# Attention results kept in SBUF, the mask moved into the product, and the scoring products in another order

## The chip, the cores and the metric

The kernel runs on one core of one Trainium2 chip. The metric is the device time in microseconds of one execution; lower is better. All data are float32.

## The reference, cut to what matters

One step of a one-layer encoder: 1024 new prompt rows and 32 sample rows with 128 cached keys. Three attention branches, a gated merge, an output projection, then PEER, which scores 128x128 product keys for each of 8 heads, keeps the best 16 experts of each row and head, gathers their rows of two tables (4 KB each) and sums them.

```python
def _mla_attend(...):                      # 8 heads, 64 + 32 dims
    s = (einsum(q_nope, k_nope) + einsum(q_rope, k_rope)) * MLA_SCALE
    s = where(k_pos // 64 <= q_pos // 64, s, -1e30)
    return einsum(softmax(s), v)

def _diff_attend(...):                     # 8 heads, two softmax maps each
    s = einsum(q, k) * DIFF_SCALE - slopes[h] * abs(q_pos - k_pos)
    s = where(chunk mask, s, -1e30);  p = softmax(s)
    return einsum(p[0] - lam * p[1], v)    # then an RMSNorm per head

def _mem_attend(...):                      # 4 heads, 256 memory tokens
    return einsum(softmax(einsum(q, mem_k) * MEM_SCALE), mem_v)

merged = g_a * (o_a @ w_br_a) + g_b * (o_b @ w_br_b) + g_m * (o_m @ w_br_m)
x = x + merged @ w_o

def _peer(h, ...):
    q = h @ wq;  sc = einsum(q, subkeys)   # (rows, 8 heads, 2 halves, 128)
    idx, g = top 16 of the 16 x 16 sums of each half's top 16, softmax
    a = gelu(einsum(u[idx], h));  return einsum(g * a, v[idx])
```

## The kernel before

Rows are worked on in tiles of 128; the sample rows are a ninth tile. `RUNS` makes three spans: tiles 0 and 1; tiles 2, 3, 4 and the sample; tiles 5, 6 and 7. Each span passes through the dense stages inputs, (memory, in the first span only), attend, merge, out and score. A stage opens on all engines when SP has seen that PE, ACT and DVE left the one before (`open_stage`, L545 and L546).

The experts are a second stream of 1056 steps, 16 for each group of 128 (row, head) pairs. In a step POOL gathers one row per partition from `peer_u` and one from `peer_v` (L594, 512 KB each, eight buffers for each table), DVE multiplies and sums (L1805), and every fourth step PE adds four weighted rows (L1968, `y_sum`). The ranking of the next group (`rank`, some twenty DVE instructions) is spread over the steps. POOL runs at most eight steps ahead of DVE and PE.

`weave` joins the two streams on PE, ACT and DVE: each dense generator yields once per tick, and after each tick the expert steps that are due by then are issued. `plan` works out how many steps are due from the costs in `ticks` and from a cap: in the scoring stage a group of 16 steps may begin only when the scores of its head are out. The first span has 21 steps in its scoring stage; the second span ends at step 321, the third at 736, and the rest runs alone.

Attention goes through jobs (pair of heads, branch, head, tile): 40, 80 and 60 in the three spans. For job j: PE writes scores to one of two PSUM buffers; DVE takes the row maximum (for the differential heads it adds the distance bias to SBUF and negates the maximum in an instruction of its own, L1356; for MLA it first writes -1e30 into a 64x64 corner, L1360); ACT takes exp; for differential heads DVE mixes the two maps; PE transposes, ACT copies to SBUF (L1297), PE multiplies by v (L1234), and `take_o` on DVE scales by the inverse sum (L1386, L1389). PE may write job j's product only when `take_o` of the job before has freed the bank (two banks in the first span). `copy_o` on ACT copies the transposed results of a pair of heads and issues their store to a DRAM scratch `oT` (L1315); SP waits for the last store before merge opens, and merge loads `oT` back beside `hT` (L1444, L1445). Two bias tables of 128x1024 are rescaled once for each pair of heads (L1429).

In the scoring stage a head's query product is two products of 256 rows of `peer_wq` columns (L1668), ACT copies each to SBUF (L1694), and then the sub-key products follow (L1679), which DVE copies out (L1709). The weights of a head (`w_q` 1 MB and `skT` 128 KB, one semaphore) have two buffers; the load for head h+2 is issued when head h's sub-key products are done:

```python
if h >= 2:
    eng.wait_ge(self.f_scored, self.f_sc0[i] + (h - 1) * sp.nt)
```

## Time and profile before

| | |
|---|---|
| median of 3 runs | 4473.66 us (4472.73 to 4478.42) |
| the profiled execution's own time | 4440.51 us, clock 0.761 |
| its span, first to last instruction | 4438.7 us |
| busy: PE, DVE, ACT, POOL | 2854.2, 2431.5, 807.9, 2377.4 us |
| DMA | 1388.83 MB, mean 313 GB/s |

The span splits into the pre-expert part (0 to 515 us), two parts in which dense stages and steps are woven (to 3400 us), and the steps alone (to 4438 us). Busy shares are averages over stages with different limits, so they are read by stage.

### The profile page before, as it was taken

What the parts mean: (1) busy time and instruction counts of PE and PEld (TensorE: products, weight loads), DVE (VectorE), ACT (ScalarE), POOL (GpSimd) and SP (SyncE); (2) the same over time, 40 slices, a digit from 0 to 9 for tenths busy, and PEclk for the clock granted to TensorE, in tenths of its full rate; (3) what the DMA queues carried; (4) which work ended last, traced back from release to release, by engine and by line L of the source; (5) the groups of instructions that cost most, each with busy time, mean ns of one, the idle gap of its engine ahead of it and who ended that gap; (6) DMA issues with size and microseconds to landing.
All of it is one profiled execution on the core that took longest, in us unless ns stands there. A gap on an engine that the chain in (4) does not pass through costs nothing.

```text
span 4438.7 us, 39034 instructions
## 1 busy us (share of the span) xinstructions
PE 2854.2 (64%) x12071; PEld 1509.4 (34%) x12071; DVE 2431.5 (55%) x6358; ACT 807.9 (18%) x1703; POOL 2377.4 (54%) x2128
## 2 busy tenths in 40 slices
PE   7779669777879965658667776896555332333333
PEld 5458445544445422334434333442222000000000
DVE  1241345377745445646488786655456565665650
ACT  1230012233321110112133332111001000000000
POOL 0000224355444346746466775675577777777774
PEclk9769879867689987879877787998777555555556
DMA  7244658788799789989899999998899999999997
GB/s 244 89 140 138 216 194 299 271 297 300 265 323 320 262 285 340 383 300 406 312 353 353 359 385 336 382 396 308 315 371 381 370 367 354 369 366 371 356 366 273
DMA packets 552141, 1388.83 MB, mean 313 GB/s; under 512 B 51296, under 2 KB 253024, under 8 KB 551936
## 3 DMA queue, kind: packets, MB, share of 16 engines
q0 software_dynamic: 304128, 1107.43, 67.1%
q1 hardware_dynamic: 227408, 249.27, 17.1%
q10 hardware_dynamic: 20400, 29.64, 2.0%
q8 instruction: 99, 1.62, 0.1%
q14 instruction: 106, 0.87, 0.1%
HBM read 1326.10 MB, written 60.05 MB: 312 GB/s over the span
## 4 chain that ended last, share of the span: by engine, by line
PE 34%; POOL 23%; issue 14%; DMA 12%; DVE 11%; ACT 2%; DVEq 2%; another core or an unknown queue 1%; SPq 1%; ACTq 0%; PEldq 0%; POOLq 0%; PEld 0%
POOL G_v_rows L594 12%; POOL G_u_rows L594 11%; PE scores L720 8%; PE scores L1479 7%; PE y_sum L1968 5%; DMA G_v_rows<-in_peer_v,G_idxT 4%; PE scores L1483 3%; DVE G_u_rows L1805 3%; PE scores L1565 2%; PE scores L1668 2%; PE o L1234 2%; DMA A_w_in<-in_w_in 2%; PE scores L1199 2%; DMA G_u_rows<-in_peer_u,G_idx 1%
## 5 line engine op out<-in xcount | busy, mean ns | idle before, releaser
L594 POOL DMA_INDIRECT G_v_rows<-in_peer_v,G_idxT x1056 | 1192.7, 1129 | 907.2 <-PE y_sum L1968 567.1
L594 POOL DMA_INDIRECT G_u_rows<-in_peer_u,G_idx x1056 | 1180.6, 1118 | 839.1 <-issue 308.2
L1805 DVE CUSTOM_DVE_ANT_0 G_u_rows<-G_u_rows,G_h 128x1024 f32<-128x1024 f32 x1056 | 1273.4, 1220 | 465.1 <-DMA G_u_rows<-in_peer_u,G_idx 420.3
L1968 PE MATMUL y_sum<-G_v_rows,G_zw 128*32 128x512 f32 x4224 | 782.9, 877 | 1000.1 <-DMA G_v_rows<-in_peer_v,G_idxT 945.6
L1968 PEld LDWEIGHTS y_sum<-G_v_rows,G_zw 128*32 128x32 f32 x4224 | 157.6, 140 | 1489.5 <-issue 1482.2
L720 PE MATMUL scores<-A_w_in,A_hT 128*128 128x256 f32 (+2 forms) x864 | 230.3, 428 | 45.0 <-DMA A_w_in<-in_w_in 30.0
L1479 PE MATMUL scores<-D_hT,D_w_gate 128*128 128x256 f32 (+2 forms) x768 | 237.5, 462 | 0.0
L720 PEld LDWEIGHTS scores<-A_w_in,A_hT 128*128 128x128 f32 x864 | 173.6, 204 | 104.0 <-DMA A_w_in<-in_w_in 27.0
L1217 PE MATMUL turn<-ident,C_probs 128*128 128x128 f32 (+1 forms) x647 | 144.0, 340 | 66.9 <-ACT C_pT L1297 44.0
L1479 PEld LDWEIGHTS scores<-D_hT,D_w_gate 128*128 128x128 f32 x768 | 144.5, 190 | 93.3 <-issue 56.1
L1709 DVE COPY F_sc<-scores 128x256 f32<-128x256 f32 x72 | 29.3, 422 | 255.8 <-PE scores L1679 184.7
L573 POOL MEMSET G_zw<- 128x1024 f32 x2 | 1.8, 957 | 293.4 <-SPq L546 293.4
L1217 PEld LDWEIGHTS turn<-ident,C_probs 128*128 128x128 f32 (+1 forms) x647 | 92.1, 178 | 168.6 <-issue 87.0
L1297 ACT ACTIVATE C_pT<-turn 128x512 f32<-128x512 f32 (+3 forms) x224 | 104.2, 465 | 242.6 <-PE turn L1217 164.9
L1479 PE MATMUL scores<-D_hT,DF_w 128*128 128x256 f32 (+2 forms) x384 | 125.3, 482 | 32.6 <-DMA D_hT<-scratch_hT 32.6
L1285 ACT ACTIVATE C_probs<-C_probs,C_ntop 128x768 f32<-128x768 f32 (+7 forms) x144 | 104.9, 729 | 212.8 <-DVE C_ntop L1356 165.9
L720 PE MATMUL scores<-A_hT,A_w_in 128*128 128x256 f32 (+2 forms) x384 | 133.4, 503 | 12.3 <-issue 12.3
L1234 PE MATMUL o<-C_v_diff,C_pT 128*128 128x64 f32 (+1 forms) x576 | 105.3, 344 | 55.9 <-DVE C_o_diff L1389 33.9
L1925 ACT ACTIVATE G_gelus<-G_dots 128x16 f32<-128x16 f32 x66 | 14.2, 216 | 677.1 <-DVEq L1809 536.9
L1668 PE MATMUL scores<-h2T,DF_w 128*128 128x256 f32 (+2 forms) x384 | 125.7, 487 | 16.2 <-DMA DF_w_br<-scratch_skT 15.8
L1512 DVE TENSOR_TENSOR D_part<-D_gate,scores 128x256 f32<-128x256 f32 (+2 forms) x48 | 25.0, 521 | 202.4 <-ACT D_gate L1498 158.9
L1668 PE MATMUL scores<-h2T,F_w_q 128*128 128x256 f32 (+2 forms) x384 | 123.7, 480 | 9.2 <-DMA F_skT<-scratch_skT 9.2
(282 smaller groups left out, 3923.5 us busy)
## 6 DMA issues: line engine op xcount, KB each, us to landing
A_w_in<-in_w_in SPq DMA_DIRECT2D x24, 1024.0 KB
D_w_gate<-in_w_gate SPq DMA_DIRECT2D x24, 1024.0 KB
G_u_rows<-in_peer_u,G_idx POOLq DMA_INDIRECT x1056
G_v_rows<-in_peer_v,G_idxT POOLq DMA_INDIRECT x1056
DF_w<-in_w_gate SPq DMA_DIRECT2D x12, 1024.0 KB
DF_w<-in_peer_wq SPq DMA_DIRECT2D x12, 1024.0 KB
F_w_q<-in_peer_wq SPq DMA_DIRECT2D x12, 1024.0 KB
G_sc<-scratch_sc ACTq DMA_DIRECT2D x66, 128.0 KB
```

The source lines that it names most:

```text
L594: pool.indirect_dma_start(out=buf[:, :], out_offset=None, in_=table, in_offset=bass.IndirectOffsetOnAxis(ap=rows, axis=0)).then_inc(signal ...
L720: last = pe.matmul(self.ps_m[n % 4][:, 0:width], lhs[c], rhs[c], start=(c == 0), stop=(c == len(lhs) - 1))
L1199: last = pe.matmul(self.ps_s[(slot + k) % 2][:, c:c + n], lhs, rhs, start=True, stop=True)
L1217: last = pe.transpose(ps_t[at % banks][0:w, b - c:b - c + P], probs[:, b:b + w], ident[:, :])
L1234: last = pe.matmul(ps_o[j % banks][:, 0:O_WIDTH[kind]], m["pT"][j % 2][0:w, b * P:(b + 1) * P], v, start=(b == 0), stop=(b == blocks - 1))
L1285: act.activation(probs[:, 0:keys], src[:, 0:keys], ACT.Exp, bias=m["ntop"][:, col:col + 1], accum_out=m["sums"][:, col:col + 1]).then_inc( ...
L1297: last = act.activation(m["pT"][j % 2][:, c:c + full], src[:, 0:full], ACT.Copy)
L1479: pe.matmul(gates[:, 0:n], m["w_gate"][b][:, c, block], m["hT"][:, c, :], start=(c == 0), stop=(c == DC - 1))
L1483: last = pe.matmul(branch[:, 0:n], m["w_br"][b][:, c, block], m["oT"][:, 4 * b + c, :], start=(c == 0), stop=(c == 3))
L1668: last = pe.matmul(self.ps_m[k % 2][:, 0:n], w[:, c, j * P:(j + 1) * P], m["h2T"][:, c, :], start=(c == 0), stop=(c == DC - 1))
L1805: dve.tensor_tensor_reduce(out=self.u_rows[slot][:, :], in0=self.u_rows[slot][:, :], in1=self.h2[t % 2][:, :], scale=1.0, scalar=0.0, op0= ...
L1968: last = pe.matmul(self.ps_y[32 * c:32 * (c + 1), cols], self.zw[b % 2][:, lo:lo + 32], self.v_rows[(4 * quad + c) % SLOTS_G][:, cols], st ...
```

## The change

- Results of attention are copied by ACT straight into the merge stage's `oT` in SBUF; the DRAM scratch, its stores, its load and SP's wait for it are gone.
- `take_o` moves from DVE to ACT. The reciprocal stays on DVE, is made for all jobs in `mix`, and waits there for the job's exp.
- The differential heads use one distance table for all heads: q is scaled by -DIFF_SCALE/slope when it is copied, the scores are shifted by the distance and scaled by the slope in one instruction that keeps the minimum, and exp is taken with scale -1. The rescaling of the bias tables and the separate negation are gone.
- The MLA mask becomes eight more rows of q and k (104 instead of 96 contraction rows); POOL makes them once and SP stores them to the scratches with 16 DMAs in the first input stage. The corner write is gone.
- In merge, out and score the ticks are finer (two per unit, three per tile, 24 instead of 16). The first three chunks of `w_o` lie elsewhere in SBUF and are loaded at the same place as before.
- In the scoring stage the first query product of head h+1 is issued ahead of the sub-key products of head h, on PE and on ACT. The load of head h+2 keeps its condition.

```diff
...
+MASKED = QK + SEQ // P
...
+def slope(h):
+    return 2.0 ** (-8.0 * (h + 1) / HEADS)
...
+            self.k_mask = self.B["subT"][0:KEY_TILES, :, :].rearrange("p b n -> p (b n)")[:, 0:KEYS]
+            self.q_mask = self.B["memT"][0:KEY_TILES, :, :, :].rearrange("p k c n -> p (k c n)")[:, 0:ROWS]
         self.experts_memory(keep)
-        with ExitStack() as ctx:
-            sb(ctx, "below_w_o", [P, BELOW_W_O])
-            self.w_o_head = [sb(ctx, f"E_w_o_head{k}", [P, D]) for k in range(W_O_HEAD)]
...
-        m["bias"] = [sb(ctx, f"C_bias{i}_{u}", [P, D]) for u in range(2)]
...
-            out += [(sp.i, "merge", 0.022 * sp.n)] * D_UNITS
-            out += [(sp.i, "out", 17.0)] * sp.nt
-            out += [(sp.i, "score", 0.016 * sp.n + 0.5 * sp.nt)] * (2 * HEADS)
+            out += [(sp.i, "merge", 0.0147 * sp.n), (sp.i, "merge", 0.0073 * sp.n)] * D_UNITS
+            out += [(sp.i, "out", 7.0), (sp.i, "out", 7.0), (sp.i, "out", 3.0)] * sp.nt
+            query, scores = (sp.i, "score", 0.016 * sp.n), (sp.i, "score", 1.0 * sp.nt)
+            out += [query] + [query, query, scores] * (HEADS - 1) + [query, scores]
...
-                out.append(max(0, min(steps, first + TOPK * max(0, heads // 2 - 1))))
+                out.append(max(0, min(steps, first + TOPK * max(0, (heads - 1) // 3 - 1))))
...
+        for u, top in ((1, P), (0, P // 2)):
+            for g in range(PAIRS):
+                pool.memset(self.q_scale[0:top, g:g + 1], -DIFF_SCALE / slope(2 * g + u)).then_inc(self.q_scaled, 1)
+            pool.wait_ge(self.q_scaled, PAIRS * (2 - u))
+        self.chunk_masks(pool)
...
+    def chunk_masks(self, pool):
+
+
+        pool.memset(self.k_mask, -1e30).then_inc(self.masks_zeroed, 1)
+        pool.memset(self.q_mask, 0.0).then_inc(self.masks_zeroed, 1)
+        pool.wait_ge(self.masks_zeroed, 2)
+        pool.affine_select(out=self.k_mask, in_=self.k_mask, compare_op=ALU.is_ge, fill=0.0, base=-CHUNK,
+                           pattern=[[1, KEYS]], channel_multiplier=-P).then_inc(self.masks_cut, 1)
+        pool.wait_ge(self.masks_cut, 1)
+        pool.affine_select(out=self.k_mask, in_=self.k_mask, compare_op=ALU.is_ge, fill=0.0, base=P - 1,
+                           pattern=[[-1, KEYS]], channel_multiplier=P).then_inc(self.masks_cut, 1)
+        for at, t in enumerate(ORDER):
+            if t < KEY_TILES:
+                rows = self.q_mask[:, at * P:at * P + CHUNK]
+                pool.affine_select(out=rows, in_=rows, compare_op=ALU.not_equal, fill=1.0, base=-t,
+                                   pattern=[[0, CHUNK]], channel_multiplier=1).then_inc(self.masks_cut, 1)
...
+            eng.wait_ge(self.masks_cut, 2 + KEY_TILES)
+            for h in range(HEADS):
+                eng.dma_start(s["kT"][h, QK:MASKED, :], self.k_mask).then_inc(self.masks_out, 16)
+                eng.dma_start(s["qT"][h, QK:MASKED, :], self.q_mask).then_inc(self.masks_out, 16)
...
-                take((name, u), m["flat"][k % 2][:, 0:sp.width], sp.width, DIFF_SCALE if name == "dq" else MEM_SCALE)
+                if name == "dq" and i == 0 and u == 0:
+                    act.wait_ge(self.q_scaled, 2 * PAIRS)
+                take((name, u), m["flat"][k % 2][:, 0:sp.width], sp.width, self.q_scale[:, u:u + 1] if name == "dq" else MEM_SCALE)
...
-                eng.dma_start(m["q_mla"][u][0:QK, :], s["qT"][2 * g + u, :, sp.cols]).then_inc(self.c_mla[u], 16)
-                load_keys(m["k_mla"][u], QK, s["kT"], 2 * g + u, self.c_mla[u])
+                eng.dma_start(m["q_mla"][u][0:MASKED, :], s["qT"][2 * g + u, :, sp.cols]).then_inc(self.c_mla[u], 16)
+                load_keys(m["k_mla"][u], MASKED, s["kT"], 2 * g + u, self.c_mla[u])
...
-        eng.wait_ge(self.c_oT_out, 48 * PAIRS * (i + 1))
...
+        def take_o(j):
+            g, kind, u, t, _, _ = jobs[j]
+            if g and j % o.n == 0:
+                act.wait_ge(self.c_turned, self.c_turn0[i] + o.o_turn[g - 1] + 3 * o.o_groups)
+            act.wait_ge(self.c_weighed, self.c_job0[i] + j + 1)
+            act.wait_ge(self.c_inverse, self.c_job0[i] + j + 1)
+            col, lo, w = 2 * (j % 4), 0 if kind == "mem" else VD * u, O_WIDTH[kind]
+            act.activation(m["o"][kind][:, sp.tiles.index(t), lo:lo + w], ps_o[j % outs][:, 0:w], ACT.Copy,
+                           scale=m["inv"][:, col:col + 1]).then_inc(self.c_taken, 1)
+
         def copy_o(g):
-            if g:
-                act.wait_ge(self.c_oT_out, 48 * (PAIRS * i + g))
             at = o.o_turn[g]
             for n, kind in enumerate(("mla", "diff", "mem")):
-                for c in range(o.o_groups):
-                    act.wait_ge(self.c_turned, self.c_turn0[i] + at + 1)
-                    k = min(o.BLOCKS, nt - o.BLOCKS * c)
-                    act.activation(m["oT"][kind][:, o.BLOCKS * c:o.BLOCKS * c + k, :].rearrange("p t n -> p (t n)"),
-                                   ps_t[at % banks][:, 0:k * P], ACT.Copy).then_inc(self.c_turn_out, 1)
-                    at += 1
-                act.wait_ge(self.c_turn_out, self.c_turn0[i] + at)
-                act.dma_start(s["oT"][g + PAIRS * n, :, sp.cols],
-                              m["oT"][kind][:, :, :].rearrange("p t n -> p (t n)")).then_inc(self.c_oT_out, 16)
+                act.wait_ge(self.c_turned, self.c_turn0[i] + at + n + 1)
+                act.activation(m["oT"][:, g + PAIRS * n, :], ps_t[(at + n) % banks][:, 0:sp.n], ACT.Copy).then_inc(self.c_turn_out, 1)
...
+            if j >= 2:
+                take_o(j - 2)
...
-                                             in1=m["bias"][u][:, lo:lo + keys], scale=1.0, scalar=-3.0e38,
-                                             op0=ALU.add, op1=ALU.max, accum_out=m["top"][:, col + k:col + k + 1]).then_inc(self.c_shifted, 1)
-                dve.drain()
-                dve.tensor_scalar(m["ntop"][:, col:col + 2], m["top"][:, col:col + 2], -1.0, None, ALU.mult).then_inc(self.c_maxed, 1)
+                                             in1=self.dist[:, lo:lo + keys], scale=slope(2 * g + u), scalar=HIGHEST,
+                                             op0=ALU.add, op1=ALU.min, accum_out=m["ntop"][:, col + k:col + k + 1]).then_inc(self.c_shifted, 1)
+                dve.drain().then_inc(self.c_maxed, 1)
                 return
-            src = self.ps_s[slot % 2]
-            if kind == "mla" and t < KEY_TILES:
-                dve.memset(src[0:CHUNK, keys - CHUNK:keys], -1e30)
-                dve.drain()
-            dve.tensor_reduce(m["ntop"][:, col:col + 1], src[:, 0:keys], AX, ALU.max, negate=True).then_inc(self.c_maxed, 1)
+            dve.tensor_reduce(m["ntop"][:, col:col + 1], self.ps_s[slot % 2][:, 0:keys], AX, ALU.max, negate=True).then_inc(self.c_maxed, 1)
...
         def mix(j):
             _, kind, _, _, keys, slot = jobs[j]
+            col, n = 2 * (j % 4), o.slots_of(j)
+            dve.wait_ge(self.c_exped, self.c_slot0[i] + slot + n)
+            dve.reciprocal(m["inv"][:, col:col + n], m["sums"][:, col:col + n]).then_inc(self.c_inverse, 1)
             if kind != "diff":
                 return
-            col = 2 * (j % 4)
             first, second = m["probs"][slot % 6], m["probs"][(slot + 1) % 6]
-            dve.wait_ge(self.c_exped, self.c_slot0[i] + slot + 2)
-            dve.reciprocal(m["inv"][:, col:col + 2], m["sums"][:, col:col + 2])
...
-        def take_o(j):
-            g, kind, u, t, _, _ = jobs[j]
-            col = 2 * (j % 4)
-            if g and j % o.n == 0:
-                dve.wait_ge(self.c_turned, self.c_turn0[i] + o.o_turn[g - 1] + 3 * o.o_groups)
-            dve.wait_ge(self.c_weighed, self.c_job0[i] + j + 1)
-            if kind != "diff":
-                dve.reciprocal(m["inv"][:, col:col + 1], m["sums"][:, col:col + 1])
-                dve.drain()
-            lo = 0 if kind == "mem" else VD * u
-            dve.tensor_scalar(m["o"][kind][:, sp.tiles.index(t), lo:lo + O_WIDTH[kind]], ps_o[j % banks][:, 0:O_WIDTH[kind]],
-                              m["inv"][:, col:col + 1], None, ALU.mult).then_inc(self.c_taken, 1)
...
-        def square_o():
-            dve.drain()
+        def square_o(g):
+            dve.wait_ge(self.c_taken, self.c_job0[i] + g * o.n + o.last["diff"] + 1)
...
-            if k >= -1 and (k + 1) % o.n == 0:
-                for u in range(2):
-                    dve.tensor_scalar(m["bias"][u][:, :], m["bias"][u][:, :], ALIBI_STEP, None, ALU.mult)
...
-        eng.dma_start(m["oT"][:, :, :], s["oT"].rearrange("c p n -> p c n")[:, :, sp.lo:sp.lo + sp.n]).then_inc(self.d_o, 16)
...
+            yield
             if unit == 0:
-                pe.wait_ge(self.d_o, 16 * (i + 1))
+                pe.wait_ge(self.c_turn_out, self.c_turn0[i] + C_OF[i].turns)
...
-        for h in range(HEADS):
-            w, skT, qT = m["w_q"][h % 2], m["skT"][h % 2], m["qT"][h % 2]
-            pe.wait_ge(self.f_w[h % 2], 32 * (HEADS // 2 * i + h // 2 + 1))
-            for j in range(2):
-                k = 2 * h + j
-                if k >= 2:
-                    pe.wait_ge(self.f_q_out, 2 * HEADS * i + k - 1)
-                for c in range(DC):
-                    last = pe.matmul(self.ps_m[k % 2][:, 0:n], w[:, c, j * P:(j + 1) * P], m["h2T"][:, c, :],
-                                     start=(c == 0), stop=(c == DC - 1))
-                last.then_inc(self.f_queried, 1)
-                if j == 0:
-                    yield
+
+        def query(h, j):
+            k = 2 * h + j
+            if j == 0:
+                pe.wait_ge(self.f_w[h % 2], 32 * (HEADS // 2 * i + h // 2 + 1))
+            if k >= 2:
+                pe.wait_ge(self.f_q_out, 2 * HEADS * i + k - 1)
+            for c in range(DC):
+                last = pe.matmul(self.ps_m[k % 2][:, 0:n], m["w_q"][h % 2][:, c, j * P:(j + 1) * P], m["h2T"][:, c, :],
+                                 start=(c == 0), stop=(c == DC - 1))
+            last.then_inc(self.f_queried, 1)
+
+        def scores(h):
+            skT, qT = m["skT"][h % 2], m["qT"][h % 2]
             pe.wait_ge(self.f_q_out, 2 * HEADS * i + 2 * h + 2)
             for t in range(nt):
                 k, r = h * nt + t, sp.rows[t]
@@ -1679,28 +1730,50 @@
                     last = pe.matmul(self.ps_m[2 + k % 2][0:r, j * P:(j + 1) * P], qT[:, j, t * P:t * P + r], skT[:, j, :],
                                      start=True, stop=True)
                 last.then_inc(self.f_scored, 1)
+
+        query(0, 0)
+        yield
+        for h in range(HEADS):
+            query(h, 1)
+            yield
+            if h + 1 < HEADS:
+                query(h + 1, 0)
+                yield
+            scores(h)
             yield
         pe.drain().then_inc(self.pe_left, 1)
...
```

## Rows read from the trace of the kernel before

**Rows 1.** Windows of seven stretches: us, busy us of each engine, granted clock, DMA share, GB/s.

```profile
...
183.00:296.00 113.00, 82.16 (x328) 59.68 (x328) 62.18 (x266) 53.32 (x176) 0.00 (x0) 0.61 0.25 74
...
850.00:1271.00 421.00, 313.78 (x1472) 183.66 (x1472) 311.00 (x926) 154.94 (x402) 211.79 (x192) 0.68 0.81 285
1271.00:1515.00 244.00, 229.92 (x784) 114.72 (x784) 108.89 (x258) 36.87 (x53) 107.43 (x100) 0.97 0.90 312
...
1594.00:1896.00 302.00, 175.95 (x736) 81.22 (x732) 168.96 (x426) 29.54 (x55) 197.97 (x167) 0.78 0.92 338
...
2184.00:2754.00 570.00, 413.89 (x2116) 224.60 (x2116) 458.91 (x1163) 195.42 (x380) 387.34 (x347) 0.75 0.98 358
2754.00:3023.00 269.00, 232.04 (x880) 118.34 (x880) 151.03 (x375) 45.75 (x67) 170.15 (x149) 0.94 1.02 379
...
3400.00:4438.00 1038.00, 324.53 (x1488) 62.42 (x1488) 572.21 (x1406) 76.19 (x147) 763.31 (x688) 0.57 0.96 356
...
```

**Rows 2.** Chain of waits, shares by line, of 183 to 296 us and 850 to 1271 us.

```profile
by line: issue 18.4%; ACT C_probs L1285 12.0%; DVE C_probs L1352 7.8%; DVE C_ntop L1362 6.3%; DVE C_probs L1376 6.0%; PE scores L1199 5.9%; ACT L1329 4.3%; DVE C_coef L1373 3.9%; DVE C_bias L1429 3.2%; DVE C_o_mla L1389 3.0%; DVE C_ntop L13
by line: issue 17.2%; PE o L1234 12.7%; PE y_sum L1968 12.6%; PE scores L1199 9.5%; DVE G_u_rows L1805 8.1%; PE turn L1217 5.7%; DVE C_probs L1352 3.8%; ACT C_probs L1285 2.5%; DVE C_probs L1376 2.5%; DVE C_ntop L1362 2.2%; PE turn L1249 1.
```

**Rows 3.** Groups by line in the whole run: busy, mean ns, idle before.

```profile
...
L1389 DVE TENSOR_SCALAR C_o_mla<-o,C_inv 128x64 f32<-128x64 f32 x64 | 18.1, 283 | 6.4 <-issue 1.7
...
L1386 DVE RECIPROCAL C_inv<-C_sums 128x1 f32<-128x1 f32 x108 | 16.8, 156 | 40.1 <-PE turn L1249 20.8 <-remote 7.9 <-issue 5.2
...
L1429 DVE TENSOR_SCALAR C_bias<-C_bias 128x1024 f32<-128x1024 f32 x24 | 15.5, 688 | 0.0
...
L1356 DVE TENSOR_SCALAR C_ntop<-C_top 128x2 f32<-128x2 f32 x72 | 13.1, 182 | 6.8
...
L1371 DVE RECIPROCAL C_inv<-C_sums 128x2 f32<-128x2 f32 x72 | 11.9, 166 | 42.3 <-ACT C_probs L1285 34.7 <-issue 6.6
...
L1389 DVE TENSOR_SCALAR C_o_mem<-o,C_inv 128x128 f32<-128x128 f32 x32 | 11.2, 351 | 2.5
...
L1300 ACT ACTIVATE C_pT<-turn 32x128 f32<-32x128 f32 x16 | 4.0, 250 | 0.0
...
```

**Rows 4.** Waits of PE in 850 to 1271 us: total, times, longest.

```profile
...
PE o L1234 <- DVE C_o_diff L1389: 23.1, 11, 5.5
PE o L1234 <- DVE C_o_mla L1389: 16.6, 5, 4.5
...
```

**Rows 5.** Waits of SP in the whole run: total, times, longest.

```profile
...
SPq L546 <- DMA scratch_oT<-C_oT_mem: 8.9, 3, 6.4
...
```

**Rows 6.** Timeline of PE in the first scoring stage: start, us, what.

```profile
...
483.27 7.07 PE L1668 MATMUL scores<-h2T,F_w_q 128*128 128x256 f32 x32
490.82 1.16 PE L1679 MATMUL scores<-F_skT,F_qT 128*128 128x128 f32 x8 [0.47 <-ACT F_qT L1694]
491.81 7.07 PE L1668 MATMUL scores<-h2T,DF_w 128*128 128x256 f32 x32
...
546.18 8.64 PE L1668 MATMUL scores<-h2T,F_w_q 128*128 128x256 f32 x32 [3.02 <-DMA F_skT<-scratch_skT]
...
```

**Rows 7.** Timeline of SP in the same stretch: issues of the sub-key loads.

```profile
...
483.88 0.58 SPq L1655 DMA_DIRECT2D DF_w_br<-scratch_skT  x1
...
534.06 0.58 SPq L1655 DMA_DIRECT2D F_skT<-scratch_skT  x1
...
```

**Rows 8.** Chain in order of time, 40 to 70 us.

```profile
...
50.92 14.99 DMA scratch_dqT<-A_flat
...
```

**Rows 9.** Timeline of SP in the first input stage.

```profile
...
52.77 0.43 SPq L658 DMA_DIRECT2D out_ckv<-A_kv  x1
...
```

**Rows 10.** Waits of PE from 466 to 1896 us.

```profile
...
PE scores L1679 <- ACT F_qT L1694: 34.2, 15, 24.1
...
```

**Rows 11.** Timeline of PE in the second scoring stage.

```profile
...
1689.40 3.59 PE L1679 MATMUL scores<-DF_w_br,F_qT 128*128 128x128 f32 x15 [3.13 <-ACT F_qT L1694]
...
```

152 lines of the change are left out of this document (97 added, 55 removed).

## The prediction

> **What bounds the kernel now.** I read the windows by stage first, then the chain of waits of single stages, the groups by line, the waits of one engine, and last the timeline where an order changes. The reader should see three kinds of stretch.
>
> The steps that run alone, 3400 us to the end, hold the DMA engines 96% busy at 356 GB/s [rows 1]. The change touches nothing there, so 1038 us stay.
>
> In the woven part the stages differ. Attention of the second span (850 to 1271 us) has the DMA at 0.81, PE busy 314 of 421 us at a mean granted clock of 0.68, DVE 311 us [rows 1]: no engine is full. Its chain goes back and forth between PE, DVE and "issue" [rows 2], and PE waits 39.7 us for DVE's `take_o` of MLA and differential jobs [rows 4]. Attention of the third span is another case: 570 us at a DMA share of 0.98, and merge behind it at 1.02 [rows 1]. There faster engines mostly wait for gathers. Merge of the second span is PE's: 229.9 of 244 us busy at clock 0.97 [rows 1]; finer ticks can't shorten it.
>
> Before the first gather nothing is DMA-bound. Attention of the first span (113 us, DMA 0.25) is a chain of short instructions [rows 1, 2], and every microsecond taken off that chain is a gain.
>
> **Part by part.** All terms are changes in us against the profiled execution's 4440.51 (span 4438.7). The median of the runs shown, 4473.66, is 33.2 above it (0.7%); I subtract the same microseconds from it.
>
> *DVE in attention.* Gone are `take_o` (0.28 us for 64 columns, 0.35 for 128), the negation (0.18) and the rescaling (0.69 each, ten a span with the first two) [rows 3]. The corner write has no row here; it is shorter than the smallest of these, so at most 0.18 for 24 jobs in each of the later spans. The reciprocal (0.16) stays. Removed from DVE: in the first span 40 x 0.3 + 16 x 0.18 + 10 x 0.69 = 22; in the second 80 x 0.3 + 32 x 0.18 + 6.9 + 4.3 = 41; in the third 60 x 0.3 + 24 x 0.18 + 6.9 + 4.3 = 33.
>
> *First span, -14.* A differential job runs around DVE, ACT and DVE, and a take of another job sits in that round with its reciprocal: 16 x (0.18 + 0.16 + 0.28) = 10, and the chain gives L1429 3.2% of 113 = 3.6 [rows 2, 3]. Bounds: -7 (only L1429 and the MLA take by their chain shares, 3.2% and 3.0%) and -22 (all).
>
> *Second span, -25.* The 41 us come off an engine that PE waits for. None of the removed lines is among the largest shares of this chain [rows 2], so they are not all on it; but the take holds PE's bank, and on ACT it comes ahead of the copy, where ACT (155 of 421 us busy [rows 1]) waits for PE anyway. Its price on ACT is bounded by 0.25 for a 32-row copy [rows 3]: 80 x 0.25 = 20 us on an idle engine, taken as hidden; without the cover it would cost those 20. Against it stands a new wait: DVE now waits for exp in 48 non-differential jobs too, and behind it in DVE's queue stand the next maximum, the expert steps and with them POOL. The row for differential jobs shows 42.3 us idle before 72 reciprocals, 0.59 each [rows 3], so at most 28 us here; in roughly half the ticks a step lies between and hides it, and I let 10 count. 41 x 0.85 - 10 = 25. Bounds: -41, and -8 (one line of 2% of the chain).
>
> *Third span, -12.* 33 us less DVE work, but only 2% of 570 = 11 us of DMA time is free; to this comes the store of 2.4 MB to `oT` (12 blocks x 128 x 384 x 4 bytes), 6.6 us at 358 GB/s [rows 1], less some wait for exp. Bounds -28 (share 1.02 as in merge, and the store) and -4.
>
> *Ends of attention, -9.* SP waited 8.9 us in total for the last stores before it opened merge [rows 5]. That goes; PE now waits for ACT's last copy, which it did before through the stage's end. The third wait, 6.4 of the 8.9, lies in the DMA-bound part, so bounds -13 (with the twelve store issues of ACT in the first span) and -4.
>
> *Merge and out, -4.* 6.5 MB of `oT` are no longer loaded; 2.4 MB of them in the stage at 1.02 are 6 us at 379 GB/s [rows 1], the others lie beside PE-bound work. Finer ticks give single microseconds in out. Bounds -12 and 0.
>
> *The mask rows.* 104 instead of 96 rows are loaded for q and k of MLA: 8 x 96 x 4 bytes x (512 + 1312 + 1408 columns) = 9.9 MB become 10.8; 0.8 MB at 358 GB/s is +2, bounds 0 and +2. The matmuls stream the same columns. The Trainium skill ("DMA: Bandwidth & Descriptors", section on why a DMA increments its semaphore by 16) says that a DMA of SP runs on the largest number of engines up to 16 that divides its slowest dimension. By that rule 96 rows use 16 engines and 104 rows 13, so the busiest engines carry a third more: 27.7 us become 37, +9 in place of +2, a rival below. No row here shows a 104-row load.
>
> *The mask's DMAs, +4.* In the first input stage 16 issues of 0.43 us [rows 9] go into SP's queue behind the memory loads and ahead of the first `dqT` store. They are 6.9 us on a queue where that store, issued at 50.92, is 14.99 us of the chain [rows 8]: ACT waits for it to reuse its buffer, and PE for ACT. Part of that landing time is the queue's backlog, which the delay doesn't lengthen. Bounds 0 and +8. POOL's mask work has no row; it lies beside 30 us of inputs.
>
> *The order of the scoring products, +18.* Here I expect a loss. The gain is PE's wait for ACT's copy: 0.47 us per head in the first span [rows 6], 34.2 us in all up to 1896 us, of which 24.1 are one stall by the first ranking, which stays [rows 10]. The cost is the cover of the weight load. The load of head h+2 is issued when head h's sub-key products end (483.88 us [rows 7]). Before, two products (7.07) and the next sub-key products (1.16) lay ahead of its first use at 491.81, which waited for nothing [rows 6]: the load took at most 7.9 us. Under gathers it took from 534.06 to 546.18, 12.1 us, and PE waited 3.02 [rows 6, 7]. After, only one product, 3.5 us, lies between. In the first span six loads are affected; that of head 4 falls into the 24 us stall. For the first two I take 7 us, for the last three 9.5 (between 7.9 and 12.1, nearer the lower as fewer gathers run in a slower stage): 2 x 3.5 + 3 x 6 = 25. After the wait of 3.02 the pair of products took 8.64 for 7.07 [rows 6], so 1 us more each: 30. Off go 8 x 0.47, the old stall of 4.6, and one product that is done ahead when the stall ends (3.5): +18. Bounds: all at 12.1 gives +39; loads of 5 us give +3.
>
> *Scoring in the second and third span, 0.* Sixteen steps lie behind most heads' sub-key products and cover the load. Only head 2's load is exposed, and the stretch without steps at the start is one product longer (about 6 us, POOL idle). Against it, waits as the 3.13 us for ACT in mid-stage go [rows 11]. The stage runs at a DMA share of 0.92 [rows 1]. Bounds -12 and +12.
>
> Sum: -14 - 25 - 12 - 9 - 4 + 2 + 4 + 18 = **-40**, so 4400.5 profiled and 4433.7 us for the median.
>
> **The rivals.** *Attention gains more* (all low bounds there): -22 - 41 - 28 in place of -51, hence 4394 us. Speaks for it PE's wait for the take [rows 4]; against, that the removed lines are small in the chain. Chance 0.12.
>
> *The DMA takes the gain*: if gathers refill every gap in the later spans, attention gives there only the store's bytes, 5.5 MB at 358 GB/s = 15 in place of 37, and with the 7 us of that in the second span half hidden, 25 less gain: 4459 us. For it the 0.98 of the third span, against it the 0.81 of the second [rows 1]. Chance 0.15.
>
> *The weight loads decide, slower than before*: the load of head h+2 arrives later than its one product in all spans. All at 12.1 in the first span is +21 over my term; in the later spans, if steps don't cover them, six loads each at 12.1 - 5.5 = 6.6 are up to +79, of which the steps hide half: 4434 + 21 + 40 = 4495 us. It turns the sign when loads add 58 us in all. For it [rows 6, 7]; against, the bursts of 16 steps. Chance 0.10.
>
> *The wait for exp decides*: 108 jobs x 0.59 = 64, all on the path in place of 10 to 15: 4434 + 51 = 4485 us. Against it, in the woven spans a step mostly lies between. Chance 0.06.
>
> *Thirteen engines for the mask rows*, the rule above: loads of 10.8 MB on the busiest engines, +7 over my term: 4441 us. Chance 0.07.
>
> **How the numbers follow.** My forecast has 0.50 and, with its bounds, 4400 to 4464. The range for 8 in 10 reaches over the other cases: 4388 to 4478. What this measurement can't tell from no change is 0.2%, about 9 us (4464.7 to 4482.6). Faster: 0.48 + 0.12 + 0.11 + 0.06 = 0.77. Same: 0.02 + 0.04 + 0.01 + 0.02 + 0.01 = 0.10. Slower: the rest, 0.13.
>
> **What would show it.** Right: the first attention near 99 us; the second at 390 to 400 with no wait of PE for a take; a wait of PE for `w_q` or `skT` before the first product of heads 2, 3, 5, 6 and 7 in the first scoring stage; merge opening at once when ACT has left; the last 1038 us unchanged. Wrong: an attention of the second span above 415 us, reciprocals on DVE that idle over 0.5 us each, or scoring of the later spans above 310 us with PE waiting for weights.

## The result, and the profile after

The changed kernel took 4439.66 us (median of 4 runs, 4430.28 to 4446.12), the kernel before 4473.19 us beside it: 33.5 us or 0.75% less. The ratio on record is 0.9922, with a 95% interval from 0.9901 to 0.9943. The prediction was 4433.7 us. On another chip, with eleven runs, the ratio was 0.9954 (0.9939 to 0.9968), 21.8 us. Its profiled execution has a span of 4428.6 us, only 10.1 less than the profiled one of before: that one ran 33 us under its kernel's median, this one 9. So the first pair of profiles shows where time went, and understates the sum.

The windows by stage of the changed kernel, the stretches that answer to [rows 1] (the same columns):

```profile
193.00:302.00 109.00, 80.80 (x334) 59.47 (x335) 43.13 (x184) 61.81 (x216) 1.85 (x2) 0.61 0.28 86
862.00:1258.00 396.00, 300.50 (x1472) 178.56 (x1472) 279.48 (x783) 172.74 (x482) 211.50 (x192) 0.71 0.85 300
1258.00:1492.00 234.00, 229.58 (x784) 114.58 (x784) 105.95 (x254) 35.58 (x52) 102.44 (x96) 0.98 0.88 304
...
2171.00:2732.00 561.00, 399.03 (x2116) 213.98 (x2116) 436.02 (x1053) 209.77 (x440) 399.38 (x348) 0.77 0.99 361
2732.00:2995.00 263.00, 231.93 (x880) 117.99 (x880) 147.22 (x363) 44.47 (x66) 160.59 (x147) 0.95 1.03 374
3390.00:4428.00 1038.00, 325.71 (x1488) 62.69 (x1488) 572.15 (x1407) 76.19 (x147) 749.90 (x686) 0.59 0.96 355
```

DVE has lost 31.5 us of work in the second span's attention (311.0 to 279.5), ACT gained 17.8. The stretches are shorter in attention, the same in the steps alone. The first window runs 2 us into merge, so attention 1 is better read from the table below. To see what each stage gave, I take from the timelines the first PE instruction of a stage and the first of the next. "c" is the pair that was profiled later on one other chip:

| stage | before | after | change | change, c |
|---|---|---|---|---|
| first inputs and memory | 175.2 | 184.2 | +9.0 | +7.5 |
| attention 1 | 117.6 | 104.5 | -13.1 | -12.5 |
| scoring 1 | 113.4 | 130.2 | +16.8 | +15.1 |
| attention 2 | 425.6 | 395.7 | -29.9 | -35.8 |
| scoring 2 | 310.9 | 326.6 | +15.7 | +10.5 |
| attention 3 | 576.3 | 562.3 | -14.0 | -5.5 |
| scoring 3, to PE's last product | 283.9 | 305.6 | +21.7 | +13.1 |
| merge and out, all three | 845.7 | 836.4 | -9.3 | -8.7 |
| inputs 2 and 3, start | 545.0 | 544.4 | -0.6 | +5.5 |
| steps alone | 1045.0 | 1038.6 | -6.4 | -15.3 |

Attention gave 57 us in the first pair and 54 in the second. Scoring took 54 and 39 of it back; 6 and 15 of that came off the steps alone, for the most part because the third scoring stage of the changed kernel holds more steps (in the second pair four: 688 matmul records of PE in it for 672). The second scoring stage holds the same steps as before, to within one. Single stages differ by up to 9 us between the two pairs (attention 3: -14.0 and -5.5).

PE's waits for the take in the second span's attention, to be read beside [rows 4] (total, times, longest):

```profile
PE o L1293 <- ACT C_o_diff L1370: 9.1, 6, 2.6
PE o L1293 <- ACT C_o_mla L1370: 8.4, 5, 3.0
PE o L1293 <- ACT C_o_mem L1370: 7.4, 3, 3.4
PE o L1293 <- issue: 17.1, 13, 4.8
```

The 39.7 us of MLA and differential jobs have become 17.5. Both views put a good part of PE's idle time ahead of this product to "issue", that is to nothing that they can name. In the kernel before this line reads:

```profile
PE o L1234 <- issue: 32.2, 13, 5.8
```

Taken together PE idled 77.3 us ahead of it before (with the 5.4 for memory jobs) and 42.0 now. The second pair, below, gives nearly the same sums, 78.8 and 41.4, and puts all of them to the take. So [rows 4] showed only half of this wait. The prediction's sign "no wait of PE for a take" didn't come: the wait has halved.

The groups by line that answer to [rows 3] (busy, mean ns, idle before):

```profile
L1426 DVE RECIPROCAL C_inv<-C_sums 128x1 f32<-128x1 f32 x108 | 17.2, 159 | 38.5 <-ACT C_probs L1344 30.8 <-issue 6.7
...
L1370 ACT ACTIVATE C_o_mla<-o,C_inv 128x64 f32<-128x64 f32 x64 | 19.4, 304 | 18.0 <-remote 12.6 <-PE o L1293 4.2 <-issue 1.0
L1370 ACT ACTIVATE C_o_diff<-o,C_inv 128x64 f32<-128x64 f32 x64 | 19.3, 302 | 32.5 <-remote 20.4 <-issue 6.4 <-PE o L1293 5.5
```

The take is 0.30 us on ACT where it was 0.28 on DVE. The reciprocals of the 108 jobs with one map now idle DVE for 38.5 us, 0.36 each, against the 0.59 of the differential ones in [rows 3]. Before, they idled it for 40.1 us, mostly for PE's turns [rows 3], so the new wait took the place of another and the total didn't grow.

The first scoring stage is where the prediction expected the loss. Timeline of PE (start, us, what, and in brackets the wait ahead of it), against [rows 6]:

```profile
482.31 3.62 PE L1718 MATMUL scores<-h2T,F_w_q 128*128 128x256 f32 x16
488.66 3.72 PE L1718 MATMUL scores<-h2T,DF_w 128*128 128x256 f32 x16 [2.73 <-DMA DF_w_br<-scratch_skT]
492.22 1.05 PE L1730 MATMUL scores<-F_skT,F_qT 128*128 128x128 f32 x8
493.11 3.62 PE L1718 MATMUL scores<-h2T,DF_w 128*128 128x256 f32 x16
499.61 3.72 PE L1718 MATMUL scores<-h2T,F_w_q 128*128 128x256 f32 x16 [2.89 <-DMA F_skT<-scratch_skT]
...
513.69 5.91 PE L1718 MATMUL scores<-h2T,DF_w 128*128 128x256 f32 x16 [6.01 <-DMA DF_w_br<-scratch_skT]
535.18 2.08 PE L1730 MATMUL scores<-F_skT,F_qT 128*128 128x128 f32 x8 [15.57 <-issue]
...
549.26 5.20 PE L1718 MATMUL scores<-h2T,F_w_q 128*128 128x256 f32 x16 [7.81 <-DMA F_skT<-scratch_skT]
...
561.60 5.41 PE L1718 MATMUL scores<-h2T,DF_w 128*128 128x256 f32 x16 [2.80 <-DMA DF_w_br<-scratch_skT]
...
574.20 3.72 PE L1718 MATMUL scores<-h2T,F_w_q 128*128 128x256 f32 x16 [2.84 <-DMA F_skT<-scratch_skT]
```

Every first product of heads 2 to 7 waits for its weights, 25.1 us in all. The 6.01 of head 4 lies in the stall by the first ranking: its product is done at 519.6, and the next one, at 535.18, needs the queries that ACT copies behind that ranking (timelines of DVE, which begins it, and of ACT):

```profile
508.67 0.49 DVE L1795 MAX8 G_best<-G_sc 128x8 f32<-128x128 f32 x2 [3.98 <-DMA G_sc<-scratch_sc]
```

```profile
534.76 0.64 ACT L1755 ACTIVATE F_qT<-scores 128x256 f32<-128x256 f32 x2
```

From the start of the ranking to this copy it is 26.1 us; in the kernel before it was 25.7, without any wait for weights (505.20 to 530.85). So head 4's load costs nothing, and 19.1 us of waits count. Counted from the stage's first product, head 3's sub-key products begin 7.3 us later than before (66.9 for 59.6), as head 2's and 3's waits and one more product now lie ahead of the ranking. The last product ends 13.7 later, and the next input stage begins 16.8 later: 3 us of the stage's growth lie behind its products.

SP issued two of these loads at:

```profile
482.51 0.37 SPq L1704 DMA_DIRECT2D DF_w<-in_peer_wq  x1
...
537.29 0.37 SPq L1704 DMA_DIRECT2D F_w_q<-in_peer_wq  x1
```

The first (head 2) was in use 6.1 us later, the second (head 5), under gathers, 12.0 us later; four of the six landed within 6.1 to 6.4.

And SP's queue in the first input stage, beside [rows 8, 9], with the step of the chain that follows:

```profile
57.74 0.51 SPq L700 DMA_DIRECT2D scratch_kT<-B_subT  x1
58.29 0.29 SPq L701 DMA_DIRECT2D scratch_qT<-B_memT  x1
58.63 0.35 SPq L727 DMA_DIRECT2D scratch_dqT<-A_flat  x1
```

```profile
58.63 17.48 DMA scratch_dqT<-A_flat
```

The store that was issued at 50.92 and took 14.99 us is issued 7.7 us later and takes 2.5 us longer. The 16 issues are 5.8 of the 7.7 (52.80 to 58.58); the queue was 1.8 behind before them. The chain names SP's mask issues one after the other from 52.80 on: they are on the path.

### The profile page after: what moved, and what is told of

Read it like the earlier page. It is cut to its first block, busy times and chain, and to the rows that moved or that the text cites. A ratio compares the mean times of both kernels' runs of the same rounds, so it can differ in the third digit from the quotient of the medians.

```text
span 4428.6 us, 38852 instructions
## 1 busy us (share of the span) xinstructions
PE 2830.5 (64%) x12071; PEld 1499.0 (34%) x12071; DVE 2352.5 (53%) x6012; ACT 846.4 (19%) x1881; POOL 2385.5 (54%) x2148
## 4 chain that ended last, share of the span: by engine, by line
PE 33%; POOL 26%; DMA 13%; issue 12%; DVE 7%; another core or an unknown queue 3%; ACT 2%; DVEq 1%; SPq 1%; ACTq 0%; PEldq 0%; POOLq 0%; PEld 0%
POOL G_v_rows L646 13%; POOL G_u_rows L646 13%; PE scores L778 7%; PE scores L1515 6%; DMA G_v_rows<-in_peer_v,G_idxT 5%; PE y_sum L2041 5%; PE scores L1520 3%; PE scores L1718 2%; PE scores L1258 2%; DVE G_u_rows L1878 2%; PE o L1293 2%; PE scores L1605 2%; DMA G_u_rows<-in_peer_u,G_idx 1%; DMA DF_w_br<-scratch_skT 1%
## 5 line engine op out<-in xcount | busy, mean ns | idle before, releaser
L646 POOL DMA_INDIRECT G_v_rows<-in_peer_v,G_idxT x1056 | 1176.5, 1114 | 929.5 <-PE y_sum L2041 561.5
L646 POOL DMA_INDIRECT G_u_rows<-in_peer_u,G_idx x1056 | 1194.3, 1131 | 813.0 <-issue 320.0
L608 POOL MEMSET G_zw<- 128x1024 f32 x2 | 1.9, 964 | 279.5 <-SPq L576 279.5
L1718 PE MATMUL scores<-h2T,F_w_q 128*128 128x256 f32 (+2 forms) x384 | 125.3, 481 | 17.5 <-DMA F_skT<-scratch_skT 17.4
L1420 DVE TENSOR_REDUCE C_ntop<-scores 128x1 f32<-128x256 f32 (+6 forms) x108 | 65.6, 607 | 119.6 <-PE scores L1258 99.1
```

Of the source, the lines that this page charges most:

```text
L646: pool.indirect_dma_start(out=buf[:, :], out_offset=None, in_=table, in_offset=bass.IndirectOffsetOnAxis(ap=rows, axis=0)).then_inc(signal ...
L1718: last = pe.matmul(self.ps_m[k % 2][:, 0:n], m["w_q"][h % 2][:, c, j * P:(j + 1) * P], m["h2T"][:, c, :], start=(c == 0), stop=(c == DC - 1))
```

## The experiments

All kernels were timed against the kernel before on their own chip (4384.7 to 4389.5 us there, 2% under the first chip), so ratios are compared, and stages within one chip where possible. Four kernels make the first group.

**The scoring stage undone.** `x_old_score` is the changed kernel with the four scoring functions, the ticks and the cap of before:

```diff
-            out += [query] + [query, query, scores] * (HEADS - 1) + [query, scores]
+            out += [(sp.i, "score", 0.016 * sp.n + 0.5 * sp.nt)] * (2 * HEADS)
-                out.append(max(0, min(steps, first + TOPK * max(0, (heads - 1) // 3 - 1))))
+                out.append(max(0, min(steps, first + TOPK * max(0, heads // 2 - 1))))
```

> The changed kernel with the scoring stage of the kernel before: its order of products, its two ticks per head and its cap; all else as changed. Between the two profiles the three scoring stages grew by 16.9, 15.8 and about 15 us, 48 in all. Theory 1, the new order costs this by itself: about 48 us off the changed kernel's 4440, so 4392. Rival, the longer stages only hold expert steps that other stages lost, and nothing is gained by going back in the later spans: only the first span's 17 us come off, 4423.

Ratio 0.9855 (0.9838 to 0.9872): 4323.1 us. By the ratios, 0.9922 and 0.9954, the changed kernel lies 29 to 43 us above this. So the scoring order with its ticks and its cap costs this much, between the rival's 17 and theory 1's 48, and less than the 54 of the first pair's stages, as part of the longer third stage comes back in the steps alone.

**The scoring stage alone.** `b_new_score` is the reverse edit on the kernel before.

> The kernel before with only the new scoring order, its three ticks per head and its cap. Theory 1: 4473 + 48 = 4521. Rival (only the first span pays): 4490.

Ratio 1.0066 (1.0053 to 1.0079), +29 us; the first scoring stage grew to 133.5 us. The cost is there without the rest of the change too. Both expected sizes were off, 48 too high and 17 too low: the first span doesn't pay alone, the later ones pay as well.

**The weight load released earlier.** In `x_split_load` the load of the query weights waits for head h's query products only. The sub-key load keeps its condition and has a semaphore of its own, for which PE now waits ahead of its sub-key products:

```diff
         if h >= 2:
+            eng.wait_ge(self.f_queried, 2 * HEADS * i + 2 * (h - 1))
+        eng.dma_start(m["w_q"][h % 2][:, :, :], ...).then_inc(self.f_w[h % 2], 16)
+        if h >= 2:
             eng.wait_ge(self.f_scored, self.f_sc0[i] + (h - 1) * sp.nt)
-        eng.dma_start(m["w_q"][h % 2][:, :, :], ...).then_inc(self.f_w[h % 2], 16)
-        eng.dma_start(m["skT"][h % 2][:, :, :], ...).then_inc(self.f_w[h % 2], 16)
+        eng.dma_start(m["skT"][h % 2][:, :, :], ...).then_inc(self.f_k[h % 2], 16)
```

> The changed kernel, but peer_wq's load for head h+2 waits only for head h's two query products (semaphore of its own), the sub-key load keeps its condition. The order of the products stays. The load is then covered by product, sub-key products and product, 8.2 us in the first span in place of 3.5. Theory 1a, the uncovered weight load is all of the cost: the first scoring stage goes back to about 114 us and the later ones to 284 and 300, so 4440 - 45 = 4395. Theory 1b, the load explains only the first span, and the later spans pay because steps and sub-key products fall otherwise (PE waited 12.9 and 16.2 us for DVE's copies of the scores there, against 2.7 and 3.7 before): about -15, 4425.

Ratio 0.9894 (0.9870 to 0.9917), 12 to 26 us under the changed kernel's: theory 1b's 15 and not 1a's 45. In the first span the waits of heads 2 to 5 are gone, those of heads 6 and 7 are still 2.80 and 2.67 us; timeline of PE, start of the same stretch:

```profile
481.87 3.62 PE L1720 MATMUL scores<-h2T,F_w_q 128*128 128x256 f32 x16
485.33 3.62 PE L1720 MATMUL scores<-h2T,DF_w 128*128 128x256 f32 x16
...
489.67 3.62 PE L1720 MATMUL scores<-h2T,DF_w 128*128 128x256 f32 x16
493.13 3.62 PE L1720 MATMUL scores<-h2T,F_w_q 128*128 128x256 f32 x16
```

**The mask's stores issued early.** In `x_mask_early` the 16 issues stand ahead of the third load of `w_in`, where SP is idle.

```diff
+        if i == 0:
+            eng.wait_ge(self.masks_cut, 2 + KEY_TILES)
+            for h in range(HEADS):
+                ...
         self.load_w_in(eng, sp, 2)
         self.load_w_in(eng, sp, 3)
```

> The changed kernel with the mask's 16 stores issued ahead of the third load of w_in, where SP stands idle from 18.4 to 32.1 us. Theory: the first input stage grew by 9.0 us because 16 issues take 5.8 us on SP's queue ahead of the first dqT store and that store lands later; then 4440 - 9 = 4431 and the stage ends near 129 us in place of 139. Rival: the masks' bytes delay other transfers wherever they are issued: no more than 2 us off.

The input stage shortened from 126.6 (`x_old_score`, same chip) to 118.4 us, and the `dqT` store is back within 1.4 us of where it was; chain of waits, 40 to 90 us:

```profile
52.35 14.29 DMA scratch_dqT<-A_flat
```

The ratio, 0.9927 (0.9914 to 0.9939), doesn't show the 8 us. The changed kernel's two ratios, from two other chips, are 0.9922 and 0.9954, 14 us apart, so how much of the 8 us reaches the end is open.

The kernels of all groups, leaving out the first chip, give the price of the scoring stage with its scatter (us; 3' is scoring 3 with the steps alone):

| | scoring 1 | scoring 2 | 3' |
|---|---|---|---|
| seven kernels with the order of before | 109.6 to 112.9, mean 111.4 | 298.2 to 304.7, mean 301.4 | 1298.4 to 1311.3, mean 1304.2 |
| four with the new order | 127.9 to 133.5, mean 130.7 | 310.8 to 316.9, mean 314.7 | 1309.1 to 1328.0, mean 1316.5 |
| `x_split_load` | 113.4 | 308.4 | 1309.4 |

The new order costs 19.3 + 13.3 + 12.3 = 45 us. With the load released earlier 2 + 7 + 5 = 14 are left. In the first span, then, the uncovered load is nearly all of it. In the later spans it is about half by one kernel, where the halves (6 and 7 us) are no larger than the scatter; the rest belongs to the order or to its ticks and cap, which were not separated. PE's waits for weights show no share of the load there: behind the first load of each span they are 0.5 and 4.1 us in `c_after`, 0 and 5.3 in `c_before`, 0 and 5.8 in `x_split_load`. One wait that took a place of its own there is PE's for DVE's copies of the scores, 12.9 us in the changed kernel's second span where it was 2.7, but in `x_mask_early` it is 3.8, and the stage is 11 us longer than in `x_old_score` all the same, so it isn't the cause. What costs the 13 and 12 us stays open.

The second group, on another chip.

> The changed kernel as it is, on one chip with the kernels of this group. In the first pair of profiles it took 10 us less than the kernel before, in the timed runs 33.5. Expected: a ratio of 0.992, and attention of the three spans shorter by 13, 30 to 38 and 14 to 27 us, scoring longer by 17, 5 to 16 and 15 to 20.

> The kernel before as it is, for a profile on the same chip. Expected: ratio 1.000; its stages, beside the changed kernel's of this group, tell how far the single stages of the first pair of profiles can be trusted.

Ratios 0.9954 and 1.0000. The stage table above has this pair in its last column: the profiled spans are 4383.9 and 4357.9, 26.0 apart, near the 21.8 of the timed runs. The stages are as expected but for the third span's, whose attention gave 5.5 us (14 to 27 expected) and whose scoring took 13.1 (15 to 20).

**The take back on DVE.** `x_take_dve` differs from the changed kernel in one instruction's engine, and with it in its place: on ACT the take stands ahead of the next copy, on DVE behind the next job's `mix`, where it stood before.

```diff
-            act.activation(m["o"][kind][...], ps_o[j % outs][:, 0:w], ACT.Copy,
-                           scale=m["inv"][:, col:col + 1]).then_inc(self.c_taken, 1)
+            dve.tensor_scalar(m["o"][kind][...], ps_o[j % len(ps_o)][:, 0:w],
+                              m["inv"][:, col:col + 1], None, ALU.mult).then_inc(self.c_taken, 1)
```

> The changed kernel with the scaling of attention's results (take_o) back on DVE, at the place it had before; reciprocals stay in mix, everything else as changed. Theory: in the first span, where the chain of short instructions runs through DVE, 40 takes of 0.3 us come back, +5 to +12; in the second span 80 takes, 24 us of DVE time, about half of it on the path, +12; third span, DMA-bound, +3: in all some 20 to 25 us slower than the changed kernel. Rival: PE waits for the take wherever it runs (in the changed kernel it waited 25 us for ACT's takes in the second span, before 45 us for DVE's), and the move is worth less than 8 us.

4393.55 us, ratio 1.0017 (0.9999 to 1.0034), 28.8 us above the changed kernel, somewhat more than the 20 to 25 expected: without this one part the change is worth nothing. Where it lies I had wrong: attention 1 +1.3 us, attention 2 +30.0 (386.2 to 416.2), attention 3 +0.8. PE's waits in attention 2, in this order: the kernel before, the changed one, the take on DVE:

```profile
PE o L1234 <- DVE C_o_mla L1389: 31.0, 12, 5.8
PE o L1234 <- DVE C_o_diff L1389: 28.5, 16, 5.5
PE o L1234 <- DVE C_o_mem L1389: 19.3, 8, 5.1
```

```profile
PE o L1293 <- ACT C_o_mem L1370: 18.9, 10, 4.8
PE o L1293 <- ACT C_o_diff L1370: 11.4, 10, 2.6
PE o L1293 <- ACT C_o_mla L1370: 11.1, 7, 3.0
```

```profile
PE o L1293 <- DVE C_o_diff L1432: 31.5, 17, 5.5
PE o L1293 <- DVE C_o_mla L1432: 30.1, 12, 5.1
PE o L1293 <- DVE C_o_mem L1432: 19.5, 9, 5.5
```

78.8, 41.4 and 81.1 us. The other removals took 13.5 us off DVE's busy time there (310.4 to 296.9), and with the take on DVE attention 2 is 416.2, against 422.0 before: they are worth 6 there, no more than such stages scatter. What PE waited for was not the 0.28 us of the take but its turn in DVE's queue. The longest wait, 5.53 us until 943.17, as DVE's timeline shows it (the lines left out are more of the same ranking, and small instructions of the next job's `mix`):

```profile
936.76 1.22 DVE L1879 CUSTOM_DVE_ANT_0 G_u_rows<-G_u_rows,G_h 128x1024 f32<-128x1024 f32 x1 [0.18 <-issue]
...
938.88 0.69 DVE L1830 TENSOR_TENSOR G_work<-ranks,G_partf 128x512 f32<-128x512 f32 x1
939.65 0.76 DVE L1835 TENSOR_TENSOR G_work<-G_work,G_pos1f 128x256 f32<-128x256 f32 x2
940.49 0.69 DVE L1837 TENSOR_REDUCE G_key<-G_work 128x32 f32<-128x512 f32 x1
...
941.95 0.88 DVE L1421 SCALAR_TENSOR_TENSOR C_probs<-C_probs,C_coef,C_probs 128x640 f32<-128x640 f32 x1
942.75 0.28 DVE L1432 TENSOR_SCALAR C_o_diff<-o,C_inv 128x64 f32<-128x64 f32 x1
```

An expert step, a piece of the ranking (938 to 941.4 us) and the next job's `mix` (to 942.75) stand ahead of the take, and PE has one bank only. Whether the take would do as well on DVE ahead of `mix` wasn't tried, so how much is the engine's and how much the place's is open. In the first span there are two banks and next to no steps, and no wait of PE is put to the take in either kernel. In the third PE waits 27.4 us for it on DVE and 9.2 on ACT, yet the stage is as long (550.9 and 550.1 us): its DMA share is 1.00 in both. The move is worth about 1 us in each.

**Both remedies.** `x_best` has scoring as before and the mask stores early.

> The changed kernel with the scoring stage of the kernel before and the mask's stores issued early. If the two gains add up: ratio 0.9855 less 9 us, 0.983 to the kernel before. Rival: the 9 us of the first input stage don't reach the end (the kernel with early stores alone had the ratio 0.9927, no better than the changed kernel's 0.9922), then 0.9855.

4319.37 us, ratio 0.9852 (0.9826 to 0.9878), and as `c_best` on the chip of the first group:

> The kernel x_best again (changed kernel, scoring as before, mask stores early), as the base of this group. Expected: ratio 0.985.

4318.33 us, 0.9842 (0.9824 to 0.9860): the two are 1.5 and 1.6% under the kernel before, and 1% under the changed one. The early stores again don't show clear of `x_old_score`'s 0.9855, as the rival has it.

The last group has `c_best` as its base.

> x_best with two edits that touch different stages, read by stage: (a) peer_wq's load for head h+2 waits only for head h's query products, with scoring in the old order; (b) DVE makes the reciprocal of the jobs of one softmax map half a job later, behind the next maximum, when their exp is done. (a): PE's remaining waits for weights in scoring go, 3 us in the first span, 0 to 5 in each later one. (b) Theory, the new wait for exp costs: attention -3 to -5 us in the first span, -10 in the second, 0 to -5 in the third. Rival: DVE has slack there, its wait only fills it, and attention stays within 2 us of the base's. Ratio to the kernel before 0.980 by the theory, 0.984 by the rival.

(a) is the split load in the old order, (b):

```diff
         def mix(j):
-            dve.wait_ge(self.c_exped, self.c_slot0[i] + slot + n)
-            dve.reciprocal(...).then_inc(self.c_inverse, 1)
             if kind != "diff":
                 return
+            invert(j)
...
             if j + 2 < len(jobs):
                 maximum(j + 2)
+            if j + 1 < len(jobs):
+                invert_late(j + 1)     # the jobs that are not differential
```

4311.07 us, ratio 0.9839 (0.9815 to 0.9863), not told apart from its base. Attention 104.1, 383.9 and 546.5 us against 104.1, 386.7 and 553.4; scoring 1 and 2 111.0 and 298.6 against 110.8 and 300.5. PE's waits for weights, but for the first load of each span, went from 5.7 us to 0.2. Two runs of the base's own code on two chips had 386.6 and 386.7, but 549.1 and 553.4 in the third span. So the wait for exp costs 0 in the first span, up to 3 us in the second, and what it costs in the third isn't told from scatter. The rival is nearer.

> x_best with the mask as before: -1e30 into the 64x64 corner on DVE, 96 rows of q and k, no mask rows made or stored. Theory: the mask in the product takes 0.18 us and a drain of DVE's path per MLA job: first attention +2, second and third +3 each, against one fewer store train in the first inputs, 0: in all +5 to +8, ratio 0.987. Rival: nothing measurable.

```diff
-MASKED = QK + SEQ // P
+MASKED = QK
+            if kind == "mla" and t < KEY_TILES:
+                dve.memset(src[0:CHUNK, keys - CHUNK:keys], -1e30)
+                dve.drain()
```

Nothing of the mask rows is made or stored, either. 4320.10 us, ratio 0.9857 (0.9840 to 0.9874) against 0.9842 (0.9824 to 0.9860), not told apart: the timed runs are with the rival. Attention 1 is 2.6 us longer, as the theory has it; 2 and 3 are 383.5 and 552.9, not longer. The mask in the product is worth those 2.6 us in the profiles; its 16 issues in SP's queue lengthened the first inputs there by three times as much.

> x_best with 112 rows of q and k instead of 104 (eight rows of zeros more, 0.8 MB more to load). By the rule in the Trainium skill's page DMA: Bandwidth & Descriptors, 104 rows run on 13 engines and 112 on 16: then the loads get shorter, the wait for the first k_mla falls under the base's and the stages of attention by up to 3 us each. Rival: the load runs on all engines either way, and 112 rows are 8% more bytes: attention 0 to 1 us longer in each span.

```diff
-MASKED = QK + SEQ // P
+MASKED = QK + 2 * (SEQ // P)
```

4312.51 us, ratio 0.9837 (0.9822 to 0.9852). PE's wait for the first `k_mla` is 39.1 us in three, the base's 39.2. The issues of the key loads themselves differ; from the tile's summaries (durations in ns, min/median/max), with 104, 96 and 112 rows (`c_best`, `x_corner2`, `x_rows112`):

```profile
L1178 SPq DMA_DIRECT2D C_k_mla<-scratch_kT x40: 365/377/1182, 185.6 to 2419.0; - x40
```

```profile
L1170 SPq DMA_DIRECT2D C_k_mla<-scratch_kT x40: 419/426/478, 184.5 to 2413.9; - x40
```

```profile
L1178 SPq DMA_DIRECT2D C_k_mla<-scratch_kT x40: 416/428/1493, 184.9 to 2410.0; - x40
```

A key load of 104 rows is issued in less time than one of 96 or of 112. A mask store takes 0.29 us with its 8 rows and 0.42 or more with the 16 rows of `x_rows112`. The loads of q don't show it as cleanly: with 96, 104 and 112 rows alike single ones take anything from 0.30 to 0.46 us. By the rule of the Trainium skill ("DMA: Bandwidth & Descriptors", section on why a DMA increments its semaphore by 16) 8, 104, 96 and 112 rows run on 8, 13, 16 and 16 engines; the issue times of stores and key loads rise in that order, 0.29, 0.377, 0.426, 0.428, which agrees with the rule, but no view here counts a load's engines. What thirteen engines cost isn't told: the wait for the first load is the same, attention 2 and 3 are 380.2 and 547.1 with 112 rows against 386.7 and 553.4, 6 us each in one profile, and the median is 5.8 us lower with overlapping intervals.

## Why the prediction was right, and where not

**The direction and the size** were right: 33.5 and 21.8 us less on two chips for 40 forecast. Part of that is luck. Attention 2 gave 5 to 11 us more than its term, merge and out 5, and these made up for part of the 25 that scoring in the later spans took where nothing was forecast.

*First attention, -14*: -13.1 and -12.5, the end included. The size holds; the move of the take, which the round of 10 us counted in, is only 1.3 of it. The corner's 16 writes, which the sum of 22 leaves out, are worth 2.6 by `x_corner2`. The rescaling and the negation weren't tried alone.

*Second attention, -25*: -29.9 and -35.8. The step "41 x 0.85 - 10" failed in its reasons. DVE lost 31 us of work and not 41. The removed work other than the take is worth about 6 us; the take's move 30, more than its busy time of some 24; the wait for exp up to 3, not 10. A take on ACT takes 0.30 us, above the 0.25 of a 32-row copy that was used as a bound. [rows 4] pointed at it: PE waited 39.7 us there, 77 with the memory jobs and what stands under "issue", and that wait, not DVE's time, was the thing to price.

*Third attention, -12*: -14.0 and -5.5, within its bounds; DMA-bound as argued: `x_take_dve` gives PE 18 us more of waits there and the stage 0.8.

*Ends of attention, -9*: here a step failed. The gap between the last product of attention and the first of merge was 8.2, 10.0 and 14.4 us and is 6.5, 10.6 and 12.2: 3 us less (3 more in the second pair), and it is inside attention's rows of the table. SP's wait is gone, but PE waits for `hT`, which is loaded when the stage opens, as before (32.6 us in all then). That merge would open at once when ACT has left was one of the prediction's signs, and it didn't:

```profile
PE scores L1515 <- DMA D_hT<-scratch_hT: 29.2, 3, 12.2
```

*Merge and out, -4*: -9.3 and -8.7, within the bounds; which of the missing load and the finer ticks gave it wasn't tried.

*The mask's DMAs, +4*: +9.0 and +7.5. The failed step is that the queue's backlog would swallow part of the delay; the store was issued 7.7 us later, 5.8 of them by the mask's issues, and took 2.5 us more. The upper bound of 8 was the value to take, and the first pair lies above it. *The mask rows, +2*: nothing that can be told.

*Scoring, first span, +18*: +16.8 and +15.1. The waits that count were forecast at 25 us and are 19.1: four of the five loads landed within 6.1 to 6.4 us, faster than the 7 and 9.5 I took, the fifth took 12.0. Head 4's wait lies in the stall and cost nothing, as forecast. What made up for the lower waits is that the ranking began one product later, so the product done ahead of it gained nothing, and 3 us behind the stage's last product, of which the sum has no term. That the sum is so close is partly luck; the mechanism is shown by `x_split_load`.

*Scoring, later spans, 0*: this is the term that failed. +13 and +12 us over the means of eleven kernels on the other chips, 25 in all, twice the upper bound. The single waits came as argued: behind each span's first load PE waits 0.5 and 4.1 us for weights in `c_after`, so the burst of 16 steps does cover the load, and the waits for ACT's copies are gone (4.9 and 4.6 us in `c_before`). The step that failed is to add up PE's waits and take the sum for the stage's change: the stages grew all the same, and the cause stays open. The prediction's sign of being wrong, later scoring stages above 310 us with PE waiting for weights, is half there: by its windows the second one went from 302 to 311 us, without the waits. The rival of the weight loads had the sign and the place, at 61 us over the forecast in all, far too dear, and its mechanism is shown in the first span only.

The rival in which the DMA takes the gain has a slip: the store of the later spans is 12 x 128 x 800 x 4 bytes = 4.9 MB and not 5.5, which moves its 4459 us by 1.

In sum: attention with its ends was forecast at -60 and gave -57.0 and -53.8; merge and out -4, and -9.3 and -8.7; the mask's DMAs and rows +6, and +9.0 and +7.5; scoring with the steps alone +18, and +47.8 and +23.4. The gain is smaller than forecast mainly by the later scoring stages. Read by its parts, one instruction's move to another engine carries the change (28.8 us, more than the whole 21.8 on that chip), and the scoring order takes back more than that.

## What to carry to other kernels

When an instruction changes its engine, price the wait that others have for it, not its duration: some 24 us of takes gave back 30 in the one stage where they queued behind other work and held the only bank, and 1 us each in the stages where nobody waited for them or the DMA was full. Look under "issue" too: 32 of the 77 us of this wait stood there. When products are reordered, count again from the condition that releases each load to its first use; a load whose release isn't moved along loses its cover, which cost 17 us in the first span here; with the old order the kernel is 66 us under the one before, with the new one 22 to 34. Issues in front of a store that lies on the path cost at least their full time in that stage (5.8 us of them lengthened it by 7.5 to 9), so put them where the queue stands idle; that this reaches the kernel's end isn't shown here.
